# Delta net: the last two levels of a triangular inverse done on their blocks

## What is computed

```python
def _gdn_chunked(q, k, v, g, beta, s0):
    ...
    gc = jnp.cumsum(g, axis=-1)
    decay = jnp.exp(jnp.where(incl, gc[..., :, None] - gc[..., None, :], -jnp.inf))
    kb = k * beta[..., None]
    lmat = jnp.where(strict, jnp.einsum('nbhid,nbhjd->nbhij', kb, k) * decay, 0.0)
    eye = jnp.eye(c, dtype=q.dtype)
    tmat = lax.linalg.triangular_solve(eye + lmat, jnp.broadcast_to(eye, lmat.shape),
                                       left_side=True, lower=True, unit_diagonal=True)
    u = tmat @ (v * beta[..., None])
    w = tmat @ (kb * jnp.exp(gc)[..., None])
    ...
```

## Time and profile before

| | us |
|---|---|
| median of 3 runs | 1543.38 |
| lowest and highest | 1539.85, 1554.34 |
| the profiled execution, its time | 1555.77 |
| its span in the profile | 1553.9 |
| busy: PE, PEld, DVE, ACT, POOL | 1414.2, 1056.7, 699.2, 415.5, 314.9 |
| mean granted clock of TensorE | 0.956 of 2.4 GHz |

### The profile page before, as it was taken

The page is one execution under the profiler, slowest core; times in us unless marked ns, Lnnn a source line. Parts: engine busy times, 40 slices in busy tenths (PEclk is TensorE's granted clock), DMA queues, the critical chain, the costliest instruction groups (busy, mean ns, idle before and its releaser), DMA issues. The chain is left out here.

```text
span 1553.9 us, 21870 instructions
## 1 busy us (share of the span) xinstructions
PE 1414.2 (91%) x8304; PEld 1056.7 (68%) x8304; DVE 699.2 (45%) x1267; ACT 415.5 (27%) x810; POOL 314.9 (20%) x450
## 2 busy tenths in 40 slices
PE   5999999999899999899798897899999999999855
PEld 1678776767898888455455446678888888888611
DVE  2656876402646663677555313543222222222246
ACT  2212021314555545333122012332222222222111
POOL 0200000102111210454342220022111112111073
PEclk9999799999999999999698996999999999999989
DMA  9645411139200000000111400179999999998787
GB/s 361 204 149 186 139 55 54 55 106 421 82 1 1 1 1 23 12 9 18 44 41 68 164 8 1 73 272 386 389 380 380 378 391 394 387 392 317 239 332 285
DMA packets 101058, 279.78 MB, mean 180 GB/s; under 512 B 22609, under 2 KB 39251, under 8 KB 99580
## 3 DMA queue, kind: packets, MB, share of 16 engines
q1 hardware_dynamic: 85148, 235.55, 41.4%
q0 software_dynamic: 15840, 43.28, 7.3%
HBM read 230.97 MB, written 64.52 MB: 190 GB/s over the span
## 5 line engine op out<-in xcount | busy, mean ns | idle before, releaser
L2663 PEld LDWEIGHTS PS<-arena 128*128 128x128 f32 x2240 | 260.1, 193 | 42.9 <-ACT arena L3147 26.3
L2663 PE MATMUL PS<-arena 128*128 128x128 f32 x2240 | 264.4, 277 | 5.2 <-DMA arena<-in_exp_w_down 3.8
L2966 DVE TENSOR_SCALAR arena<-PS,arena 128x1024 f32<-128x1024 f32 x70 | 89.9, 1284 | 141.5 <-PE PS L2671 141.5
L2671 PE MATMUL PS<-arena 128*128 128x512 f32 x280 | 137.8, 614 | 0.8 <-DVE arena L2959 0.8
L844 PE MATMUL PS<-arena 128*128 128x320 f32 x384 | 111.4, 445 | 1.5 <-DVE arena L1257 1.5
L849 PE MATMUL PS<-arena 128*128 128x320 f32 x384 | 107.3, 432 | 0.0
L3153 ACT ACTIVATE arena<-PS 128x128 f32<-128x128 f32 x70 | 19.4, 278 | 313.8 <-PE PS L2663 313.8
L2959 DVE TENSOR_TENSOR arena<-arena,PS 128x128 f32<-128x128 f32 x70 | 20.1, 288 | 184.1 <-ACT arena L3153 184.1
L844 PEld LDWEIGHTS PS<-arena 128*128 128x128 f32 x384 | 74.4, 196 | 33.1 <-issue 5.1
L849 PEld LDWEIGHTS PS<-arena 128*128 128x128 f32 x384 | 73.0, 190 | 30.4
L857 PE MATMUL PS<-arena 128*128 128x256 f32 (+1 forms) x400 | 89.7, 383 | 0.0
(11 more groups left out here) (467 smaller groups left out, 2199.8 us busy)
## 6 DMA issues: line engine op xcount, KB each, us to landing
arena<-in_exp_w_gate SPq DMA_DIRECT2D x70, 512.0 KB, 6.0
arena<-in_exp_w_up SPq DMA_DIRECT2D x70, 512.0 KB, 9.1
arena<-in_exp_w_down SPq DMA_DIRECT2D x70, 512.0 KB, 16.9
y_rows<-arena SPq DMA_DIRECT2D x70, 512.0 KB, 17.0
y_rows<-cst SPq DMA_DIRECT2D x1, 21504.0 KB, 58.4
arena<-in_w_in SPq DMA_DIRECT2D x16, 1024.0 KB, 5.8
arena<-in_w_mod SPq DMA_DIRECT2D x32, 512.0 KB, 3.6
arena<-in_w_mod SPq DMA_DIRECT2D x4, 2048.0 KB, 15.1
```

The source lines that it names most:

```text
L2663: mm = pe.matmul(PS[:, bank, 0:P], w[:, k, :], xT[j % 2][:, k, :], start=k == 0, stop=k == KT - 1)
L2671: mm = pe.matmul(PS[:, 4 + 2 * (j % 2) + half, :], hid[j % 2], ed[j][:, 512 * half:512 * half + 512], start=True, stop=True)
L2966: dve.tensor_scalar(yb[j].rearrange("p (h n) -> p h n", h=2), PS[:, 4 + 2 * (j % 2):6 + 2 * (j % 2), :], gate_col[j % 2], None, ALU.mult). ...
```

## The change

At levels 5 and 6 only the blocks that these levels touch are computed. `halves_of(d, n)` lists the pairs of neighbouring blocks of size s = 2^n (two pairs of 32 at level 5, one pair of 64 at level 6), with first and second half exchanged for the backward direction. For each pair and head the two products become matmuls of s by s by s, written to the block's partitions and columns. The masked product becomes a plain copy of the blocks that were computed (two copies of 32 partitions by 4x32 at level 5, one of 64 by 4x64 at level 6). Inverse_out copies only the new off-diagonal blocks; the rest of `gTT` stands there from before. The turns after levels 4 and 5, which feed levels 5 and 6, are plain matmuls with the identity on the diagonal blocks that are read next (two of 32 by 32 per head, then one of 64 by 64), and turned_out copies those blocks. Levels 1 to 4 and everything else stay.

```diff
--- before.py
+++ after.py
@@ -361,6 +361,20 @@
         def rev(i, n, x):
 
             return 2 * LAST_N * i + 2 * n + x + 1
+
+        BLOCK_LEVEL = 5
+
+        def halves_of(d, n):
+
+            s, out = 1 << n, []
+            for m in range(P // (2 * s)):
+                first, second = slice(2 * s * m, 2 * s * m + s), slice(2 * s * m + s, 2 * s * (m + 1))
+                out.append((second, first) if d else (first, second))
+            return out
+
+        def columns(h, part_):
+
+            return slice(P * h + part_.start, P * h + part_.stop)
 
         def split_tile(t):
 
@@ -890,15 +904,25 @@
                             pe.wait_ge(g_at, nth(i, x))
                     else:
                         pe.wait_ge(g_tt, lev(i, n, x))
-                    for h in range(4):
-                        mm = pe.transpose(PS[:, bank_a(x), P * h:P * h + P], gTT[x][:, h, :], ident)
+                    if n + 1 >= BLOCK_LEVEL:
+                        for a, b in halves_of(UNITS[2 * i + x][0], n + 1):
+                            for h in range(4):
+                                mm = pe.matmul(PS[a, bank_a(x), columns(h, a)], gTT[x][a, h, a], ident[a, a], start=True, stop=True)
+                    else:
+                        for h in range(4):
+                            mm = pe.transpose(PS[:, bank_a(x), P * h:P * h + P], gTT[x][:, h, :], ident)
                     mm.then_inc(g_tr, 1)
 
                 def level_first(i, n, x):
 
                     pe.wait_ge(g_t, rev(i, n - 1, x))
-                    for h in range(4):
-                        mm = pe.matmul(PS[:, bank_a(x), P * h:P * h + P], gMT[x][:, h, :], gT[x][:, h, :], start=True, stop=True)
+                    if n >= BLOCK_LEVEL:
+                        for a, b in halves_of(UNITS[2 * i + x][0], n):
+                            for h in range(4):
+                                mm = pe.matmul(PS[b, bank_a(x), columns(h, a)], gMT[x][a, h, b], gT[x][a, h, a], start=True, stop=True)
+                    else:
+                        for h in range(4):
+                            mm = pe.matmul(PS[:, bank_a(x), P * h:P * h + P], gMT[x][:, h, :], gT[x][:, h, :], start=True, stop=True)
                     mm.then_inc(g_lv1, 1)
 
                 def level_second(i, n, x):
@@ -906,9 +930,15 @@
                     pe.wait_ge(g_p, lev(i, n, x))
                     if n == 1 and i > 0:
                         pe.wait_ge(g_staken, nth(i - 1, x))
-                    for h in range(4):
-                        mm = pe.matmul(PS[:, bank_b(x), P * h:P * h + P], gPm[x][:, h, :], gTT[x][:, h, :],
-                                       start=n == 1 and h == 0, stop=h == 3, skip_group_check=True)
+                    if n >= BLOCK_LEVEL:
+                        for a, b in halves_of(UNITS[2 * i + x][0], n):
+                            for h in range(4):
+                                mm = pe.matmul(PS[a, bank_b(x), columns(h, b)], gPm[x][b, h, a], gTT[x][b, h, b],
+                                               start=False, stop=h == 3, skip_group_check=True)
+                    else:
+                        for h in range(4):
+                            mm = pe.matmul(PS[:, bank_b(x), P * h:P * h + P], gPm[x][:, h, :], gTT[x][:, h, :],
+                                           start=n == 1 and h == 0, stop=h == 3, skip_group_check=True)
                     mm.then_inc(g_lv2, 1)
 
                 def mlstm_row(i, y):
@@ -1471,7 +1501,11 @@
                     mask = strict[:, 1 - d, LV - 1 - n, :]
                     dve.wait_ge(g_lv1, lev(i, n, x))
                     src = heads(PS[:, bank_a(x), :])
-                    if n == 1:
+                    if n >= BLOCK_LEVEL:
+                        for a, b in halves_of(d, n):
+                            j = dve.tensor_copy(gPm[x][b, :, a], src[b, :, a])
+                        j.then_inc(g_p, 1)
+                    elif n == 1:
                         dve.wait_ge(g_pmi, nth(i, x))
                         dve.copy_predicated(gPm[x], spread(mask.bitcast(U32), 1, 4), src).then_inc(g_p, 1)
                     else:
@@ -1898,13 +1932,25 @@
                                        ACT.Copy).then_inc(proj_taken, 1)
                 def inverse_out(i, n, x):
                     act.wait_ge(g_lv2, lev(i, n, x))
-                    act.activation(gTT[x], heads(PS[:, bank_b(x), :]), ACT.Copy).then_inc(g_tt, 1)
+                    whole = heads(PS[:, bank_b(x), :])
+                    if n >= BLOCK_LEVEL:
+                        for a, b in halves_of(UNITS[2 * i + x][0], n):
+                            j = act.activation(gTT[x][a, :, b], whole[a, :, b], ACT.Copy)
+                        j.then_inc(g_tt, 1)
+                    else:
+                        act.activation(gTT[x], whole, ACT.Copy).then_inc(g_tt, 1)
 
                 def turned_out(i, n, x):
                     act.wait_ge(g_tr, rev(i, n, x))
                     if n == 0:
                         act.wait_ge(g_qd, nth(i, x))
-                    act.activation(gT[x], heads(PS[:, bank_a(x), :]), ACT.Copy).then_inc(g_t, 1)
+                    turned = heads(PS[:, bank_a(x), :])
+                    if n + 1 >= BLOCK_LEVEL:
+                        for a, b in halves_of(UNITS[2 * i + x][0], n + 1):
+                            j = act.activation(gT[x][a, :, a], turned[a, :, a], ACT.Copy)
+                        j.then_inc(g_t, 1)
+                    else:
+                        act.activation(gT[x], turned, ACT.Copy).then_inc(g_t, 1)
 
                 def mlstm_exps(i, y):
                     d, t, s = UNITS[2 * i + y]
```

## The result

The changed kernel takes 1561.5 us (median of 4 runs, 1556.5 to 1572.4) against 1542.8 us for the kernel before (4 runs, 1539.9 to 1554.3). The ratio is 1.0115, with a 95% interval from 1.0069 to 1.0162: slower by about 18 us, where 1538 us had been forecast, within a range that ended at 1556.

The account below looks back on a forecast made before the run. TensorE, near full, was taken as the bound, with ScalarE setting level 5. Five pairs at 1.1 us less made 5.5 us, 1555.8 to 1550.3 us profiled, 1538 us by the runs' median; range 1528 to 1556.

Parts of the forecast that it names:

- The sum: Over the five pairs: 1.1 us less each, 5.5 us in all, from 1555.8 to 1550.3 us in the profiled execution.
- The rival of the clock: In level 5 of each pair the clock falls: +7 to +14 us against -5.5, so 1545 to 1552; chance 0.12.
- TensorE's pace in small groups: In levels 5 and 6, time from record to record: 30 ns for 32 columns and 57 ns for 64.
- The rival in which loads aren't hidden: In small blocks a load isn't hidden behind the matmul before: +6.3 us a pair, +32 us, 1575; chance 0.10.
- Price of a change of shape: Where TensorE goes between groups of different block shape: 0.15 us a change.
- step 3: Turn after level 5, with mLSTM's state between two changes of shape: level 6 begins 0.33 us late.
- Step 1: Turn after level 4: 0.48 us for 0.47 and 0.42, plus one change of shape; level 5 begins 0.25 us later.
- Step 2: Level 5: TensorE saves 1.9 us, none of it counts since ScalarE isn't free; turn begins at 504.25, before 504.23.
- Step 4: Level 6: with its products in blocks u_and_w begins at 509.55 instead of 510.63, 1.1 us less a pair.

## Why the prediction failed

The step that failed is the clock. The sum held it at 1.00 in the pairs and put its cost at nothing; the rival that had it fall got 0.12 and a price of 1.4 to 2.8 us a pair. It fell in all five pairs, at an estimated 4.5 us each. What the sum says of the work itself came out nearly as forecast.

- **The rival of the clock** went wrong in three ways. Its cause was read as rest: from the earlier trace rows I compared the busy time of the new level 5 (1.75 of 3.5 us) with that of a stretch that had kept its clock (1.77 of 3.4). TensorE's matmuls in that stretch were all 128 by 128. The kernel with two heads has rests too and keeps its clock; the one with the rest filled by small blocks loses it. Its chance was then too low. And its size: I took 2.8 us at the lower level for a fall, once or twice, from the one fall in the pairs of the trace, which a full-size level 1 followed. The window of 3.9 us ahead, in the same rows, has a clock of 0.85: the fall had begun there, and lasted 3.4 us. In the changed kernel a fall lasts 10 to 14 us. Without falls its pairs should be near the 235.8 us of level 6 alone, since level 5 takes the same 7.1 us either way, and they take 258.1: that gives 22 us for the five falls (an estimate).
- **TensorE's pace in small groups**: right. 16 loads of 32 by 32 take 0.48 us, the last one's own 0.11 in it, so a mean of 25 ns a record. Inside one block the loads start 31 ns apart, for the 30 taken; only where the next pair of blocks follows do two start side by side. For 64 by 64 inside one block it is 57 ns, as taken (8 loads in 0.54 us in the kernel with level 6 alone, the last one's 0.14 in it), and 47 on average where two blocks follow each other (32 loads in 1.58 us). The rival in which loads aren't hidden is out. The Trainium skill, page "TensorE: Matmul & The Clock Gate", section "Packing small matmuls — row/col tiling", says that a load overlaps only with matmuls of another row group; here four heads in a row use one block of the array, and a load of 108 ns begins every 31, so the trace does not agree. Another sentence of that section also lets a load go ahead into a background weight buffer, which these rows don't contradict.
- **Price of a change of shape**: taken at 0.15 us, and about right for most. At full clock the kernel with level 6 alone leaves 0.07 us free between the 64 by 64 turn and mLSTM's state and 0.12 behind the state, where full groups overlap by 0.03 and 0.09: 0.3 us for the two, as taken in step 3. From the small turn to mLSTM's output it is less, 0.04 us free (503.68 to 503.72). Step 1 forecast level 5 to begin 0.25 us later; it begins where it did, 2.95 us behind the first turn in both, as its first loads start beside the last ones of the turn.
- **Step 2** (ScalarE sets level 5, nothing is won there): right. Inverse_out is right behind the exponentials (L1968 is their last line, L1938 inverse_out), and the turn stands 7.11 us behind the first one for 7.07. Two copies of 32x128 take 0.55 us for the 0.49 taken.

```profile
508.45 1.24 ACT L1968 ACTIVATE arena<-PS,arena 64x128 f32<-64x128 f32 x4
509.71 1.12 ACT L1938 ACTIVATE arena<-PS 32x128 f32<-32x128 f32 x4
```

- **Step 4** (level 6): right, where the clock holds. Taken alone it gave 5.0 us in five pairs, with full turns 6.4, against 5.5 forecast.
- **Range**: its upper end of 1556 us was to hold the rival of the clock, and that had +14 us at most. With 22 us for the falls and 5 for the gain the same sum gives the 17 that the pairs lost; but the 22 is taken from these pairs, so that is no test of it.

The Trainium skill says in the same page's Part 1 ("The HAM clock gate") that the gate goes by how busy TensorE has been recently. Taken as busy time, the runs do not agree: with small blocks the clock fell behind 5.72 busy us of 6.37, and with full ones it held through 5.58 of 6.66. What the runs do show is an order. With 32 by 32 in level 5 and 64 by 64 in level 6 the pairs have some 62 us at the lower level; with the same columns over 128 rows, 21; with 64 by 64 in level 6 alone, or in the products of levels 3 to 5, 3.4, as before; with half the heads in full size, none. That this is activity of the array, to which a small block adds little, fits all of them but is argued.

## What to carry to other kernels

A matmul cut to its useful block is faster by itself and can make its neighbours slower: before cutting, ask whether the stretch's clock may be held up by the work that is to go, and look at the granted clock behind the cut, not only at the groups that were cut. Cut only where TensorE's time is on the path (level 6 here, and not level 5, where ScalarE had covered all of it). Where a block must be small, running it over all 128 rows with zeros cost no time here and gave back part of the clock.

## What was unexpected of the hardware

- Busy share doesn't foretell the granted clock: over the five pairs 0.87 at 95% busy (32 by 32 blocks filling the rest), 1.00 at 93% (half the heads in full size).
- Rows of the contraction count in it at equal time: 3.4 to 7 us at the lower level for 10 to 14, with the same 117 records in the same 7.1 us.
- How long the clock stays down differs with what follows: 10 to 14 us in the changed kernel, where 64 by 64 blocks follow, and 3.4 to 7 us where full ones do (only level 5 small). It is no fixed time: with only the products small, falls of 3.4 and of 14 us stand in one trace. What exactly is counted, and why the kernel with quarter-size products ends 0.5% later although its pairs don't, stays open.
